# Two-layer hybrid diffusion backbone on one Trainium2 core: one activation function table, loaded once and kept

## The reference

```python
h = rms_norm(x, g_norm1) * (1.0 + sc1) + sh1
z = split(h @ w_in)                    # 12 slots of 256 columns
o_a = global attention(z): rms_norm and rotary on q and k, softmax over 768 keys
o_b = window attention(z): the same with a sink logit
o_c = GLA(z):   log_sigmoid gates, chunked linear attention, rms_norm * silu(r)
o_d = mLSTM(z): log_sigmoid gates, exponentials, rms_norm * sigmoid(o)
x = x + ga1 * (concat(o_a, o_b, o_c, o_d) @ w_out)
h = rms_norm(x, g_norm2) * (1.0 + sc2) + sh2
x = x + ga2 * (square(relu(h @ w_mlp1)) @ w_mlp2)
```

## Time and profile before

| | |
|---|---|
| median of 3 runs | 1971.44 us (1968.79 to 1973.38) |
| profiled execution | 1965.84 us |
| its span, first to last instruction | 1963.7 us |
| granted TensorE clock, mean | 0.959 of full speed |
| TensorE busy | 1775.0 us, 90% |
| VectorE busy | 1116.5 us, 57% |
| ScalarE busy | 827.9 us, 42%, 1094 instructions |
| GpSimd busy | 379.4 us, 19% |

### The profile page before, as it was taken

How to read it: one execution, slowest core, us unless ns; L and a number is a source line. 1 busy time by engine, 2 the same in 40 slices (tenths; PEclk the granted TensorE clock), 3 DMA queues, 4 the chain that set the end, 5 groups by cost and what they waited for, 6 DMA issues and landing times.

```text
span 1963.7 us, 27860 instructions
## 1 busy us (share of the span) xinstructions
PE 1775.0 (90%) x11328; PEld 1531.6 (78%) x11328; DVE 1116.5 (57%) x1638; ACT 827.9 (42%) x1094; POOL 379.4 (19%) x124
## 2 busy tenths in 40 slices
PE   5898998888897899999999968999788979999998
PEld 3687896666786889999999857877567758787776
DVE  3373746576536797787987936564566542212132
ACT  4442328643326634535435454325752352223230
POOL 0132621200210000000000013351100423443432
PEclk7899999999998999999999979999999989999999
DMA  8630111100054517547275132212200113222221
GB/s 321 202 137 22 66 44 67 64 1 1 1 193 193 215 66 296 207 165 298 82 267 214 43 109 100 80 67 74 86 2 1 66 63 107 85 88 101 89 86 64
DMA packets 33856, 217.61 MB, mean 111 GB/s; under 512 B 4660, under 2 KB 5082, under 8 KB 15322
## 3 DMA queue, kind: packets, MB, share of 16 engines
q1 hardware_dynamic: 33754, 216.19, 29.7%
HBM read 196.77 MB, written 19.40 MB: 110 GB/s over the span
## 4 chain that ended last, share of the span: by engine, by line
PE 68%; DVE 12%; ACT 8%; issue 6%; DMA 3%; POOL 2%; SPq 0%; DVEq 0%; ACTq 0%; POOLq 0%
PE ps L2341 24%; PE ps L2770 19%; PE ps L2513 6%; PE ps L2328 3%; PE ps L2595 1%; DMA raw<-w_modl 1%; DMA first_mod<-w_modl 1%; DVE xT L2073 1%; PE ps L2710 1%; POOL w_lo L697 1%; PE ps L2285 1%; DVE w_lo L2033 1%; PE ps L2446 1%; PE ps L2641 1%; DVE mx L1786 1%
## 5 line engine op out<-in xcount | busy, mean ns | idle before, releaser
L697 POOL TENSOR_TENSOR w_lo<-raw,w_hi 128x2048 fp32r<-128x2048 f32 x64 | 295.5, 4617 | 1252.8 <-ACT w_hi L801 1252.8
L2770 PE MATMUL ps<-op_hi,w_hi 128*128 128x384 f32 x896 | 306.9, 342 | 20.5 <-DVE xT L2073 6.7
L2770 PE MATMUL ps<-op_lo,w_hi 128*128 128x384 f32 x896 | 303.9, 339 | 0.0
L2770 PE MATMUL ps<-op_hi,w_lo 128*128 128x384 f32 x896 | 303.8, 339 | 0.0
L801 ACT ACTIVATE w_hi<-raw 128x2048 fp32r<-128x2048 f32 x64 | 122.1, 1908 | 189.3 <-PE ps L2341 130.5
L2770 PEld LDWEIGHTS ps<-op_hi,w_hi 128*128 128x128 f32 x896 | 170.4, 190 | 28.4 <-issue 16.7
L2341 PE MATMUL ps<-h_hi,w_hi 128*128 128x512 f32 x496 | 167.9, 381 | 3.6 <-POOL w_lo L697 3.6
L2770 PEld LDWEIGHTS ps<-op_hi,w_lo 128*128 128x128 f32 x896 | 170.1, 190 | 0.0
L2770 PEld LDWEIGHTS ps<-op_lo,w_hi 128*128 128x128 f32 x896 | 170.1, 190 | 0.0
L2341 PE MATMUL ps<-h_lo,w_hi 128*128 128x512 f32 x496 | 163.3, 372 | 0.0
L2341 PE MATMUL ps<-h_hi,w_lo 128*128 128x512 f32 x496 | 162.4, 370 | 0.0
(11 more groups left out here) (353 smaller groups left out, 3703.3 us busy)
## 6 DMA issues: line engine op xcount, KB each, us to landing
raw<-w_big SPq DMA_DIRECT2D x96, 1024.0 KB, 4.8
raw_m<-w_modl SPq DMA_DIRECT2D x20, 1024.0 KB, 5.9
raw<-w_modl SPq DMA_DIRECT2D x16, 1024.0 KB, 4.9
op_hi<-op_cache SPq DMA_DIRECT2D x21, 768.0 KB, 4.6
op_lo<-op_cache SPq DMA_DIRECT2D x21, 768.0 KB, 6.1
first_mod<-w_modl SPq DMA_DIRECT2D x8, 1024.0 KB, 19.2
x_keep<-xT SPq DMA_DIRECT2D x2, 3072.0 KB, 14.0
xT<-x_keep SPq DMA_DIRECT2D x2, 3072.0 KB, 9.9
```

Of the source, the lines that this page charges most:

```text
L697: nc.gpsimd.tensor_tensor(w_lo[r][:], raw[raw_r][:], w_hi[r][:].bitcast(F32), ALU.subtract).then_inc(sem("lo_ready"), 1)
L2770: ins = mm(bank(base + g, 0, h), wide(w)[:, k, g * P:(g + 1) * P], ops[hl][:, k, 0:h], start=(p in FRESH and k == 0 and q == 0), stop=(k = ...
```

## The change

ScalarE's program begins with one load of a table that holds logarithm, exponential and square. The four one-column logarithms and their tile go. `norm` is written shorter with the same instructions.

```diff
@@ build
-    tbl = keep("tbl", [2])
@@ scalar program
+            nc.scalar.preload_act_table_set("natural_log_exp_and_others")
             act.wait_ge(sem("v_cols"), 1)
             nc.scalar.activation(cs[:, :, 0], vcol[0][:, V_C:V_C + KD], ACT.Exp, scale=-1.0)
@@ norm_mlp
-                nc.scalar.activation(tbl[:, 0:1], eps[:], ACT.Ln)
                 act.wait_ge(sem("ms_ready"), T_("ms").add())
@@ norm
-                if l == 1 and which == 1:
-                    rstd(slice(0, HALF), bank(4, 0, HALF))
-                else:
-                    nc.scalar.activation(tbl[:, 0:1], eps[:], ACT.Ln)
-                    rstd(slice(0, n_t), bank(4, 0, n_t))
+                rstd(*((slice(0, HALF), bank(4, 0, HALF)) if l == 1 and which == 1 else (slice(0, n_t), bank(4, 0, n_t))))
```

## The result

The changed kernel took 1946.27 us, median of 5 runs (1942.74 to 1947.97), beside 1970.56 for the kernel before (1966.05 to 1973.38, 5 runs). The ratio is 0.988, with a 95% interval of 0.9862 to 0.9898. The medians differ by 24.3 us; 26.1 were predicted, and 1945 us.

A forecast was written before the change was run, and what follows sets the result against it. TensorE, busy 90% of the span, was taken as the bound, so ScalarE's loads count only where TensorE waits. 5.5 + 5.0 + 5.6 + 4.9 + 0.8 + 2.6 + 1.3 + 0.4 = 26.1 us saved, hence 1945; range 1938 to 1955.

The forecast's parts named there:

- Roots and sigmoid: Roots and first sigmoid of each layer: TensorE's and VectorE's stops behind the loads go, 5.5 us in layer 0, 5.0 in layer 1.
- Attention: Sigmoid inside the attention: without two loads the next `prob` starts earlier and the clock recovers; 5.6 us layer 0, 4.9 layer 1.
- I expect no fall after it: Attention of layer 0: the stop shrinks to 1.3 us and the clock stays full behind it, counted as 2.4 us.
- The rival in which the clock doesn't come back: TensorE's lower clock may come from work before the stop; 5.6 us fall out, 20.5 saved, 1951 us; chance 0.13.
- `norm_mlp`: Three loads, 3.85 us, on ScalarE's path; a weight block's DMA landing takes their place, leaving 0.8 us.
- Norm between the layers: Two loads, each holding back an Exp and the chain behind it, in series: 2.6 us.
- Norm before the last MLP: One load, at 1577.43, stands ahead of everything: 1.3 us.
- Gates of layer 1: TensorE waits for VectorE, which still gets stuck behind POOL's subtraction: 0.4 us, bounded by 0 and 5.6.
- In the MLP quarters ... nothing is gained or lost: No load ran in the MLP quarters of either layer, so the change there is 0.
- the likeliest case: The forecast itself: 22 to 31 us saved, chance 0.66.
- The two rules of the Trainium skill: Logarithm then exponential count as one load, so gain 0; 1.38 us of draining per load, so 9.7 us more.

The follow-up runs named there:

- the kernel with the sigmoid in three: The changed kernel with the three activations of the attention's sigmoid set at three pairs, one at each, rsqrt_mean and the multiplication one pair later; 1941.87 us, ratio 0.9863.
- the last pair: The changed kernel with norm_mlp's copies together and the attention's sigmoid spread over three pairs, without and with the unused tile `tbl`: 1939.50 and 1933.40 us.
- the first pair of profiles: Profiles of the changed kernel (1946.27 us) and of the same kernel with the tile `tbl` still allocated and never used (1939.73 us).

## Why the prediction was right, and where it was not

The time, 1945 against 1946.27, and the range hold, and putting the loads back shows that the sum was right for its reasons, stage by stage and within some 3 us. That the total came within 1.3 us is partly luck. The prediction had no term for the places of the tiles, which took 4 to 7 us away; with the tile left in place the change saves 29.7 us by the means, 3.6 more than the forecast's 26.1.

- **Roots and sigmoid: right.** 5.5 forecast, 5.6 in layer 0 and 5.6 lost again with the loads back. In layer 1 5.0 forecast, 4.0 to 4.1 by the profiles, 5.25 in the kernel with the sigmoid in three (35.20 us), where the clock is low at one place fewer.
- **Attention: the stops right, the clock half.** With the loads back in both layers 11.1 us by the means, 10.5 forecast. In layer 1 4.4 of 4.9, with the clock full behind the sigmoid. In layer 0 the profile has 1.9 of 5.6, and the profiles of the others without loads there 1.9 to 4.3. The step that failed is "I expect no fall after it": behind 1.35 us the clock fell to 0.59 (2.4 us were counted for its coming back), and it fell at two more places (338 to 342, 392 to 398). The rival in which the clock doesn't come back was right for layer 0 alone.
- **`norm_mlp`: the mechanism right,** 0.0 and 0.9 for 0.8 in the two profiles of the changed kernel, up to 1.9 in those of the others. The landing took the loads' place; moving the copy brought 3.75 us out.
- **Norm between the layers: a little undersized,** 2.6 forecast, 3.4 measured, 3.5 lost with the loads back, 2.4 to 3.9 over all profiles without loads there. Where the 0.8 us beyond the two loads come from was not traced. **Norm before the last MLP:** 1.3 forecast, 1.6 measured, 2.8 with the loads back.
- **Gates of layer 1: not contradicted by the runs** (0.4 forecast, loads back: nothing measurable; by the two profiles the stage lost 2.1), with VectorE stuck as reckoned: the small scan that took 4.70 us at 1219.43 takes 0.41, and others are stuck in its stead, six scans of `bb` for 6.38 us (2.00 without) and two products for 6.35. VectorE's timeline in the changed kernel:

```profile
1190.34 6.38 DVE L1661 TENSOR_TENSOR_SCAN bb<-ones,pre 128x128 f32<-128x128 f32 x6
...
1197.61 2.00 DVE L1661 TENSOR_TENSOR_SCAN bb<-ones,pre 128x128 f32<-128x128 f32 x6
...
1207.49 0.41 DVE L1699 TENSOR_TENSOR_SCAN ft<-ones,ft 4x128 f32<-4x128 f32 x1
1208.37 6.35 DVE L1558 TENSOR_TENSOR ex<-ft,ex 128x768 f32<-128x768 f32 x2
```

- **"In the MLP quarters ... nothing is gained or lost": wrong.** 3.3 us were gained in layer 0 and 1.4 lost in layer 1. Of the edit I had priced the four instructions on `tbl` and not the tile. Its removal cost 4 to 7 us in the whole (4.4 and 7.2 by the means with the tile back, not timed beside the changed kernel itself; 6.1 in the last pair, timed side by side). Of this 2.8 us are TensorE's stop at the gates of layer 1, where VectorE's first product got stuck instead of the second. What comes beside it goes with the clock and is not the same each time: 3.2 us at the roots of layer 1 in the first pair of profiles, 0.2 in the last. The 29.7 us with the tile left in place (mean 1940.3, from 1970.0 timed beside it) lie near the upper end of the likeliest case.
- **The two rules of the Trainium skill,** page "ScalarE: Activation LUTs". That a logarithm and an exponential share one load ("Table sets: the hidden batching unit") came true once the program named the set: one load, where 65 stood before. The 1.38 us of draining ("What ACT_TABLE_LOAD costs") are in no run here. The page states them for a switch to a different set, which the loads put back are not; but 0.01 to 0.03 us lie between a load and its neighbours in these and in those of the kernel before alike.

What stays open is why 32 bytes change the pace of a matmul. That a shift of 0.3 us between GpSimd and VectorE then decides over 2.8 us of TensorE's stop is in the traces. What brings that shift, and why the clock at the roots of layer 1 is full in two of the three kernels with the tile, is not.

## What to carry to other kernels

Price a removed instruction by the stop that it stands behind, and prove it by putting it back in one stage at a time: 8 loads were worth some 11 us, 32 others 9, 12 more nothing. When a load leaves a queue, look at what next holds that queue (here a landing, 3.84 us for 3.85), and move that as well. When an edit frees a tile, keep its place in a first comparison: the addresses of all that follows change, and that alone was 4 to 7 us here.

## What the hardware showed that was not expected

- Tiles 32 bytes further on: 336 products of TensorE in 59.23 us instead of 58.79, 59.23 in two other profiles with the tile as well, 58.79 in the changed kernel's second one; and layer 1's MLP in 360.8 instead of 362.2.
- The granted clock of the same instructions differs with when they begin: 0.55 and 1.00 in the same ten microseconds of two kernels that are alike there, 5.5 us over the attention and mLSTM. A profiled execution can stand 5 us from its kernel's median (1947.39 against 1941.96), so a single pair of profiles can be off by that much in the total. Single stages repeat better in two profiles of one kernel, to within 0.2 us in most of them.
- Which of GpSimd and VectorE starts first, by 0.3 us, decides which of VectorE's products takes 5 us instead of 0.9, and so whether TensorE stops for 5.3 us or for 2.5.
- A load of the table that is in place is not skipped: 1.28 us like any other.
